# One Trainium2 core, two transformer blocks: part of the odd column tile's projection moved into the stage before it, gate columns streamed instead of held, first norm's scaling moved to ScalarE, recurrence rows begun two steps later

## The reference, cut to what matters

```python
h = rmsnorm(x, g_mix_pre)                       # TokenNorm
proj = h @ w_in                                 # PairProj
qa, ka, va, gate_a, beta_a, alpha_a, ... = split(proj)
beta = sigmoid(beta_a)                          # 4 columns   (GdnGates)
g = -exp(a_log) * softplus(alpha_a + dt_bias)   # 4 columns   (GdnGates)
...
f = (silu(h @ w_gate) * (h @ w_up)) @ w_down    # GatedPairs, then TokenPairs + TokenRows
# second block, twice:
proj = x_in @ w_in_2                            # PairProj, 29 column tiles
y = rwkv(...); y = group_norm(y) * gate         # Rwkv, then RwkvOut (rows of the recurrence)
a = gqa(...); n = na(...)                       # Attention, Attention
x = layer_norm(ALPHA * x + gate * (mix @ w_out_2))   # TokenPairs + TokenRows
```

## Time and profile before

| what | value |
|---|---|
| median of 3 runs | 4882.77 us (4880.57 to 4890.25) |
| the profiled execution's own time | 4876.77 us |
| its span in the profile | 4875.0 us |
| PE busy | 4541.5 us, 93% |
| DVE / ACT / POOL busy | 56% / 30% / 20% |
| mean granted TensorE clock | 0.971 of full |

### The profile page before, as it was taken

How to read it: one execution, slowest core, us unless ns; L and a number is a source line. 1 busy time by engine, 2 the same in 40 slices (tenths; PEclk the granted TensorE clock), 3 DMA queues, 4 the chain that set the end, 5 groups by cost and what they waited for, 6 DMA issues and landing times. The chain is left out here.

```text
span 4875.0 us, 96946 instructions
## 1 busy us (share of the span) xinstructions
PE 4541.5 (93%) x41054; PEld 2881.5 (59%) x41054; DVE 2716.3 (56%) x4643; ACT 1465.8 (30%) x2452; POOL 976.6 (20%) x1174
## 2 busy tenths in 40 slices
PE   7998989899999989998999888998999899989897
PEld 4445955444444445554999855654544499976563
DVE  3763466785432336765545366566676545446656
ACT  1222353100000113332223255543343132336552
POOL 0002311000100000001233233530000132315460
PEclk9999999999999999999999899999999899999999
DMA  2332021343424544444121111213444411111122
GB/s 90 114 98 96 2 78 70 122 152 112 159 87 165 181 133 149 144 163 147 54 61 55 37 48 40 74 61 113 136 162 169 143 55 48 55 37 55 51 73 82
DMA packets 344923, 471.84 MB, mean 97 GB/s; under 512 B 39799, under 2 KB 247959, under 8 KB 343536
## 3 DMA queue, kind: packets, MB, share of 16 engines
q1 hardware_dynamic: 292416, 267.83, 17.7%
q0 software_dynamic: 52080, 197.81, 11.6%
HBM read 330.50 MB, written 148.65 MB: 98 GB/s over the span
## 5 line engine op out<-in xcount | busy, mean ns | idle before, releaser
L473 PE MATMUL psum<-arena 128*128 128x512 f32 x2352 | 1034.1, 596 | 14.0 <-POOLq L222 7.1
L3226 PE MATMUL psum<-arena 64*64 64x64 f32 (+5 forms) x23040 | 907.0, 232 | 25.0 <-POOL arena L3196 9.9
L3226 PEld LDWEIGHTS psum<-arena 64*64 64x64 f32 (+3 forms) x23040 | 867.3, 143 | 66.6 <-issue 23.3
L473 PEld LDWEIGHTS psum<-arena 128*128 128x128 f32 x2352 | 446.9, 191 | 562.8 <-issue 543.2
L1033 PE MATMUL psum<-arena 128*128 128x512 f32 x1344 | 582.1, 594 | 12.4 <-DVEq L222 5.3
L688 PE MATMUL psum<-arena 128*128 128x512 f32 x1232 | 535.6, 594 | 4.5 <-DVE arena L754 2.7
L2597 DVE CUSTOM_DVE_ANT_0 arena<-psum,arena 128x512 f32<-128x512 f32 (+3 forms) x532 | 292.8, 588 | 310.9 <-PE psum L2484 290.7
L1033 PEld LDWEIGHTS psum<-arena 128*128 128x128 f32 x1344 | 254.1, 190 | 330.7 <-issue 318.2
L688 PEld LDWEIGHTS psum<-arena 128*128 128x128 f32 x1232 | 232.0, 190 | 301.5 <-issue 291.7
L3430 DVE TENSOR_TENSOR arena<-arena,psum 128x384 f32<-128x384 f32 x320 | 177.9, 556 | 332.2 <-PE psum L3226 298.7
L2484 PE MATMUL psum<-arena 64*128 64x512 f32 (+3 forms) x1192 | 274.4, 546 | 91.3 <-DVE arena L2597 68.3
(11 more groups left out here) (341 smaller groups left out, 5217.0 us busy)
## 6 DMA issues: line engine op xcount, KB each, us to landing
arena<-w_in SPq DMA_DIRECT2D x86, 512.0 KB, 5.7
proj<-arena SPq DMA_DIRECT2D x172, 256.0 KB, 2.0
arena<-w_mod POOLq DMA_DIRECT2D x24, 1024.0 KB, 5.7
arena<-proj POOLq DMA_DIRECT2D x34, 640.0 KB, 5.1
arena<-down_sum SPq DMA_DIRECT2D x40, 512.0 KB, 3.7
arena<-proj SPq DMA_DIRECT2D x28, 640.0 KB, 6.9
arena<-w_down SPq DMA_DIRECT2D x30, 512.0 KB, 3.6
x_home<-arena POOLq DMA_DIRECT2D x26, 512.0 KB, 4.2
```

What stands on the lines that cost most here:

```text
L473: ins = pe.matmul(ps[:, b, :], L[:, k, :], R[:, k, :], start=(p in ("P1", "P5", "P6", "P7") and k == 0), stop=(k == KT // 2 - 1), skip_gro ...
L3226: return pe.matmul(out, lhsT, rhs, start=first, stop=last, skip_group_check=not (first and last))
```

## The change

Five edits. In both PairProj stages of the second block, the first two of the lone tile's three products (tokens 256 to 767, and now the context tokens) are issued by the TokenPairs stage ahead, after its last product and before the rest of its side work; they wait for the evictions of the token tiles they read and for their weights. In TokenNorm the multiplication `zs` goes from DVE to ACT. The gate columns become the stationary operand: 16 matmuls of 512 moving tokens, the first four contraction blocks into PSUM partitions 0 to 7 and the other four into 64 to 71, then two copies by ACT into a cleared buffer, then 8 matmuls that add the two halves and turn them; the side work has 6 steps instead of 4, and the pace is raised by as many. The recurrence rows beside the grouped attention take no step in main steps 0 and 1, then two, and three in steps 2, 8, 14, 20, and so on.

```diff
-            for kind in ("11", "12") + (("x",) if first else ()):
+            self.parts = (("11", first, 512), ("x", 0, first), ("12", first + 512, 512))
+            for kind, _, _ in self.parts:
                 store(-1, kind, [self.alone[1]])
...
+            for i, (kind, at, n) in enumerate(self.parts):
...
+    def odd(self, pe, i):
+
+        _, at, n = self.parts[i]
+        pe.wait_ge(*self.weights["alone", 0])
+        for k in range(KT):
+            ins = pe.matmul(self.c.psum[:, i, 0:n], self.chunk(2)[:, k, :], self.x[:, k, at:at + n],
+                            start=(k == 0), stop=(k == KT - 1))
+        ins.then_inc(self.s_pe.sem, 1)
+
+    def first_products(self, pe):
+
+
+        for sem, value in self.early_tokens:
+            pe.wait_ge(sem, value)
+        for i in range(2):
+            self.odd(pe, i)
+
     def run_pe(self, pe):
         ps, E, A, Dv = self.c.psum, self.s_pe, self.s_act, self.s_dve
         first = self.first
         if self.alone:
-            pe.wait_ge(*self.weights["alone", 0])
-            for i, (n0, n1) in enumerate(((first, first + 512), (first + 512, first + 1024), (0, first))):
-                for k in range(KT):
-                    ins = pe.matmul(ps[:, i, 0:n1 - n0], self.chunk(2)[:, k, :], self.x[:, k, n0:n1],
-                                    start=(k == 0), stop=(k == KT - 1))
-                ins.then_inc(E.sem, 1)
+            for i in range(3):
+                if i == 2 or not self.early_tokens:
+                    self.odd(pe, i)
                 yield
...
             act += [f"sd{i}"] if i < n else []
+            act += [f"zs{i - 1}"] if 0 < i <= n else []
             dve += [f"ss{i}"] if i < n else []
-            dve += [f"zs{i - 1}"] if 0 < i <= n else []
+            dve += [f"ri{i - 1}"] if 0 < i <= n else []
...
-            pe.wait_ge(Dv.sem, Dv.at(0, f"zs{t}"))
+            pe.wait_ge(A.sem, A.at(0, f"zs{t}"))
...
+            if 0 < i <= self.n:
+                t = i - 1
+                act.wait_ge(Dv.sem, Dv.at(0, f"ri{t}"))
+                act.activation(self.zs[:, t % 2, :], self.rows[:, t, :], ACT.Copy, scale=self.st[:, t, 1:2]).then_inc(A.sem, 1)
...
                 dve.wait_ge(A.sem, A.at(0, f"sd{t}"))
                 dve.reciprocal(self.st[:, t, 1:2], self.st[:, t, 1:2])
-                dve.drain()
-                dve.tensor_scalar(self.zs[:, t % 2, :], self.rows[:, t, :], self.st[:, t, 1:2], None, ALU.mult).then_inc(Dv.sem, 1)
+                dve.drain().then_inc(Dv.sem, 1)
...
+        if self.next_products:
+            self.next_products(pe)
+
+    def turned(self, t):
+
+        last, r = self.passes - 1, self.rows
+        return [(r.s_act.sem, r.s_act.at(0, f"ev{t}")), (r.s_dve.sem, r.s_dve.at(0, f"ev{t}")),
+                (self.s_act.sem, self.s_act.at(0, f"c{last}_0_11")), (self.s_dve.sem, self.s_dve.at(0, f"c{last}_0_12"))]
...
+        self.sum, self.two = buf[:, 224:224 + SEQ], buf[:, 224 + SEQ:232 + SEQ]
+        self.s_pool = Steps(core.pool, "clear", 1)
...
-        self.steps = 4
-        self.s_pe = Steps(core.pe, "proj", 1)
-        self.s_act = Steps(core.act, "beta expa abs exp ln", 1)
+        self.steps = 6
+        self.s_pe = Steps(core.pe, "halves proj", 1)
+        self.s_act = Steps(core.act, "copy beta expa abs exp ln", 1)
         self.s_dve = Steps(core.dve, "biased pos g", 1)
 
     def run_pool(self, pool):
         pool.dma_start(self.wb, self.w).then_inc(self.c.moved[0].sem, 16)
+        ident = self.c.const("ident")
+        pool.memset(self.sum, 0.0)
+        pool.tensor_tensor(self.two, ident[:, 0:8], ident[:, 64:72], ALU.add)
+        pool.drain().then_inc(self.s_pool.sem, 1)
 
     def run_pe(self, pe):
         yield
         pe.wait_ge(self.c.moved[0].sem, self.loaded)
+        for s in range(2):
+            for k in range(KT // 2):
+                for j, at in enumerate((0, 64)):
+                    ins = pe.matmul(self.c.psum[at:at + 8, s, :], self.wb[:, 4 * j + k, :], self.hT[:, 4 * j + k, 512 * s:512 * s + 512],
+                                    start=(k == 0), stop=(k == KT // 2 - 1), skip_group_check=True)
+        ins.then_inc(self.s_pe.sem, 1)
+        yield
+        yield
+        pe.wait_ge(self.s_act.sem, self.s_act.at(0, "copy"))
         for n in range(GN):
-            for k in range(KT):
-                ins = pe.matmul(self.c.psum[:, 0, 8 * n:8 * n + 8], self.hT[:, k, n * P:(n + 1) * P], self.wb[:, k, :],
-                                start=(k == 0), stop=(k == KT - 1))
+            ins = pe.matmul(self.c.psum[:, 2, 8 * n:8 * n + 8], self.sum[:, n * P:(n + 1) * P], self.two, start=True, stop=True)
         ins.then_inc(self.s_pe.sem, 1)
 
     def run_act(self, act):
+        yield
+        yield
+        act.wait_ge(self.s_pe.sem, self.s_pe.at(0, "halves"))
+        act.wait_ge(self.s_pool.sem, self.s_pool.at(0, "clear"))
+        for at in (0, 64):
+            ins = act.copy(self.sum[at:at + 8, :], self.c.psum[at:at + 8, 0:2, :].rearrange("p a b -> p (a b)"))
+        ins.then_inc(self.s_act.sem, 1)
         yield
         yield
         yield
         v4 = lambda a: a.rearrange("p (n h) -> p n h", h=GH)
         act.wait_ge(self.s_pe.sem, self.s_pe.at(0, "proj"))
-        z = self.c.psum[:, 0, 0:64].rearrange("p (n c) -> p n c", c=8)
...
         yield
         yield
+        yield
+        yield
         v4 = lambda a: a.rearrange("p (n h) -> p n h", h=GH)
         dve.wait_ge(self.s_pe.sem, self.s_pe.at(0, "proj"))
-        z = self.c.psum[:, 0, 0:64].rearrange("p (n c) -> p n c", c=8)
+        z = self.c.psum[:, 2, 0:64].rearrange("p (n c) -> p n c", c=8)
...
-                        late=(0, 1, 2, 13, 14, 15, 21, 22, *gates) if last else ())
+                        late=(0, 1, 2, 13, 14, 15, 21, 22, *gates) if last else (), early_tokens=prod.turned(5 if last else 3))
+        prod.next_products = gemm.first_products
...
-        gqa.pace = lambda n: 2
+        gqa.pace = lambda n: 0 if n < 2 else 2 + (n % 6 == 2)
...
-        gemm.beside = [GdnGates(side, hT, w_in[:, :, 16 * P:16 * P + 8], pcol("gates", 0, 8), beta, g, R(big + 64, 224)),
+        gemm.beside = [GdnGates(side, hT, w_in[:, :, 16 * P:16 * P + 8], pcol("gates", 0, 8), beta, g, R(rest, 232 + SEQ)),
...
-        gemm.pace = lambda n: n < 6 or (n >= 16 and (n % 2 == 0 or n >= 88))
+        gemm.pace = lambda n: n < 8 or (n >= 16 and (n % 2 == 0 or n >= 88))
```

More of the change, by code:

```diff
@@ L271, with __init__ @@
              ("P2", 0, "A12", "B21"), ("P3", 1, "S4", "B22"), ("P4", 3, "A22", "T4"))
-    def __init__(self, core, w, tiles, x, first, out, room, eighth=(), silu=(), late=(), keep=False):
+    def __init__(self, core, w, tiles, x, first, out, room, eighth=(), silu=(), late=(), keep=False, early_tokens=()):
         super().__init__(core)
+        self.early_tokens = early_tokens
         self.w, self.out, self.x, self.first, half = w, out, x, first, KT // 2
@@ L390, in sp @@
             row = self.alone[1]
-            for i, (kind, at, n) in enumerate((("11", self.first, 512), ("12", self.first + 512, 512), ("x", 0, self.first))):
+            for i, (kind, at, n) in enumerate(self.parts):
                 if i == 2:
@@ L486, in run_act @@
         if self.alone:
-            for i, (kind, n) in enumerate((("11", 512), ("12", 512), ("x", self.first))):
+            for i, (kind, _, n) in enumerate(self.parts):
                 act.wait_ge(E.sem, E.at(0, f"alone{i}"))
@@ L922, in __init__ @@
             core.unit_used[j % 8] = self.s_pe.at(0, f"{self.ORDER[x % 7][0]}_{x // 7}_{c}" if sums else f"P4_{self.passes - 1}_0")
-        self.steps = 7 * C * self.passes
+        self.steps, self.next_products = 7 * C * self.passes, None
     def end(self, x, p):
@@ L3768, in row_of, with second_block @@
     return src[i:i + 1, :].broadcast_to([n, src.shape[1]])
-def second_block(nc, core, a, p2, fac, ms, gate_rows, h, h_at, x_home):
+def second_block(nc, core, a, p2, fac, ms, gate_rows, h, h_at, x_home, prod):
     R = core.region
@@ L3992, in program @@
         prod.pace = lambda n: n in (3, 4) or 36 <= n < 48 or n >= 78
-        second_block(nc, core, a, p2, fac, ms, gate_rows, h, h_at, x_home)
+        second_block(nc, core, a, p2, fac, ms, gate_rows, h, h_at, x_home, prod)
         core.stages = core.stages[first:upto]
```

## The result

The changed kernel takes 4905.86 us (median of 5 runs, 4902.28 to 4911.75), the kernel before 4881.02 (5 runs, 4878.82 to 4890.25): a ratio of 1.0049, interval 1.0034 to 1.0064. It is 25 us slower. I had forecast 4867 with a range up to 4880, and gave slower 6 in 100. The forecast was wrong in sign.

What follows compares the result with a forecast made beforehand. PE, busy 93% of the span, was taken as the bound. Terms 3.3 - 16.5 - 4.7 - 14.3 + 1 + 15 = -16.2 us from 4876.8 give 4860.6; the median stands 6.0 above: 4867 us, range 4849 to 4880.

Steps and rivals of the forecast that it cites:

- Gates and first norm: Gate columns ahead of layer 1's projection gain 16.5 us; TokenNorm's multiplication on ACT costs 3.3 us.
- Rival (1): Gate columns: the column halves don't run at once, 7.0 us of the gain go, 4874 us; chance 0.14.
- rival (5): PE's saved time is given back at the next barrier and the gates bring nothing: 4883 us, no change; chance 0.04.
- PE's 19.5 us shrink to 7.0, less 0.2: 12.3: Behind layer 2's boundary PE owes less after early products; with 2.0 us of wait removed, gain 14.3 us.
- its like for layer 1: Behind layer 1's boundary PE owes 7.0 us instead of 19.4, with the stage ending at 1785.5, not 1778.0: gain 4.7 us.
- Rival (3): Both boundaries give half: weights come with the last load, transposes behind early products delay barriers; 10 us lost, 4877; chance 0.08.
- Recurrence rows, layer 2: Layer 2's grouped attention: DVE waits some 10 us for its rows, fourth main step near 4399; +15 us, bounds +3 and +22.
- rival (4): Layer 2's attention: the wait leaves TensorE at 1.2 GHz for several units, +30 us, 4897 us; chance 0.05.
- +5 for the steps made up later and their grouping: Layer 2's grouped attention: 5 us for catching up delayed recurrence steps, added to 10 us of stall, +15 together.
- Rival (2): Layer 2's attention does not stall, as POOL loads early or DVE's work covers it: -12 us, 4855; chance 0.19.
- Recurrence rows, layer 1: Layer 1's grouped attention: DVE's 6.7 us stall goes, but steps bunch in some main steps; +1 us, bounds -4 and +4.
- 5 gained and 6 paid: Layer 1's grouped attention: 5 us from the stall gone, 6 us lost to bunched and made-up steps, net +1 us.

Runs made afterwards that it cites:

- the run with one set of partitions: Gates edit with both halves' products in the same eight PSUM partitions, using two more banks, against the kernel before: 4874.81 us, ratio 0.9983.
- the gates alone: Kernel before with only the gate columns' stage replaced by the new one: 4866.61 us, ratio 0.9967.
- the run with the meeting moved and the preparation held back: Kernel before with early lone-tile products, band stage's meeting at 8 main steps instead of 5, recurrence preparation two main steps later: 4868.49 us, ratio 0.9976.
- the tails alone: Kernel before with only the lone tile's first products run early, in the row work's tail ahead of both barriers: 4886.32 us, ratio 1.0006.
- the pairs: Kernel before with recurrence rows two steps later, owed steps caught up in two pairs of neighbouring units: 4902.68 us, ratio 1.0047.
- the load in time: Kernel before with recurrence rows two steps later, their first loads issued at the attention stage's head, ahead of the additions: 4903.68 us, ratio 1.0055.
- the run with the band meeting moved alone: Kernel before with only the band stage's meeting put off from 5 to 8 main steps behind its DMA: 4882.7 us, ratio 1.0006.
- the run with the tails and the meeting moved: Kernel before with early lone-tile products and the band stage's meeting put off from 5 to 8 main steps: 4875.18 us, ratio 0.999.

## Why the prediction was wrong

**Gates and first norm: right.** -15.0 against -16.5, and +3.7 against +3.3, the 1.5 us being the first product's scatter; the halves take 7.04 us for the 7.0 forecast, the join 1.85 for 1.8, and the slow stretch is gone. Rival (1) is refuted by the run with one set of partitions, rival (5) by the gates alone.

**The boundaries: the step that failed.** It is the sentence "PE's 19.5 us shrink to 7.0, less 0.2: 12.3", and its like for layer 1. It takes each microsecond that PE owes less behind the barrier as a microsecond of time. I followed ACT's copies and DVE's right sums behind the barrier, and not the side lane, which has its meeting in PE's queue a fixed number of main steps on and a 28.6 us transfer behind it. Its row was there to be read before: POOL at 1808.46, 29.1 us at line 222, 30.45 us behind the barrier, on the very step to which I let PE come 12 us earlier. Between the changed kernel and the run with the meeting moved and the preparation held back lie 5.3 + 3.3 = 8.6 us in layer 1 and 10.6 - 0.9 = 9.7 in layer 2; between the tails alone and that run, which differ in nothing else, lie 16.6 us of the medians taken against the kernel before (+5.1 and -11.5). That is what the missed meetings cost, the waits and the lower clock behind them together. The rest of the miss, 1.4 and 3.7, is size; the barriers came 1.8 and 1.5 us later than I had them. Rival (3) named two other reasons for half a gain: the weights landed early, as I forecast, and the transposes behind the products are the 6.8 to 9.3 us by which the barrier of layer 1 moved, which I had counted.

**Recurrence rows, layer 2: right mechanism, two terms too small.** The place and length of the stall were right (10.07 us, the fourth step at 4398.87). Its price was not 10 but 13.6 (11.1 once the pairs are in: 289.6 to 278.5). PE comes out of it slow: the row sums at 0.95 us a record (3.78 for 4) and the scores behind at 0.52 in place of 0.28, which I had left to rival (4). "+5 for the steps made up later and their grouping" is the term furthest off: the stage is 13.1 us over with the load in time (284.7 against 271.6), 6.2 of which the pairs take away (284.7 to 278.5). The other 6.9 I can't assign; that the fewer steps in the first two units leave DVE idle there and crowded later would fit, but no run separates it. Rival (2), no stall, falls with the 10.07 us. Rival (4) came nearest to the time, with 4897, and that is luck: it wanted 30 us from a slow clock, and PE's busy time, where a slow clock shows, is 6.4 us longer.

**Recurrence rows, layer 1: "5 gained and 6 paid".** The wait of 6.7 us went as forecast, and about 12 were paid. The 6 I had put down were for PE waiting at steps that now lie together. What the windows show is PE's pace: 7.0 us more busy time at the lower level, a term that I had at nothing. Grouping is part of the loss: in pairs the stage is 2.7 us over in place of 8.5. Why the clock falls more often there is open.

Of the 44.7 us between the forecast for the profiled execution (4860.6) and what it took (4905.3), the boundaries are 10.0 + 13.4, the attentions 4.3 + 11.5, gates and norm 1.9, scatter the rest.

## What to carry to other kernels

Before counting PE time saved behind a barrier as gained, list every wait in PE's queue behind it with the distance of its releaser from the barrier, side lanes and long transfers included: a wait that shows 0 us now has a slack (3.7 and 3.3 us here), and the slack is the most that the edit can bring. When such a wait is moved, look at what the late engine does next; here the load behind the transfer took over at once. Work laid beside a pipeline has a place in each unit: with the owed steps made up singly at every sixth unit, the same instructions cost 6 to 9 us more in one stage than with the steps made up in pairs.

## What the runs showed of the hardware

A granted clock of 1.00 in a window is a reading only where the trace holds records of the clock. The first product of the first projection is the same 8 instructions in every kernel with an unchanged norm; here it is in the kernel before and in the run with the band meeting moved alone, whose code is the same up to there:

```profile
49.11 3.70 PE L473 MATMUL psum<-arena 128*128 128x512 f32 x8 [1.27 <-DVEq L222]
```

```profile
49.52 6.76 PE L473 MATMUL psum<-arena 128*128 128x512 f32 x8 [1.27 <-DVEq L222]
```

3.70 and 6.76 us, and 5.51 in the gates alone, while the window of that product reads 1.00 there (49.4 to 54.9). But the trace's first record of the clock lies at 47.3 us in the kernel before, at 53.1 in the gates alone and at 55.7 in the run with the meeting moved. It is a record of the full level each time, and with no record ahead of it the window is printed as if the clock were full. In the gates alone the product's records start 0.85 to 1.01 us apart before 53.1 and 0.43 apart from 53.5 on; in the run with the meeting moved all of them start before 55.7 and lie 0.85 us or more apart. In the run with the tails and the meeting moved, 0.85 us a record is also the pace of such records where the clock is on record as 0.50 (3434.0 to 3438.4). So the first product ran at the pace of the lower level until the first record, and when that came differed: between 47.3 and 55.7 us in the twelve profiles with an unchanged norm, one of each kernel. Up to 3 us at this place is chance, and a forecast from one execution has to carry it.
